# Attention probabilities normalised by the product that turns them, the first head pair's keys and values made in the mixer's last tile, and a new hand-written order of the mixer

## The reference, cut to what matters

```python
q = einsum('bsl,lhe->bshe', rms_norm(c_q), w_uq)          # 64 plain + 32 rotary columns a head
ckv = rms_norm(c_kv); kpe = apply_rope(k_pe)
kv = einsum('bsl,lhe->bshe', ckv, w_ukv)                  # keys (64) and values (64) of each head
s = (q_nope @ k_nope + q_pe @ k_pe) * MLA_SCALE           # 64-token chunks, causal by chunk
o = softmax(s) @ v
...
y, state = wkv_scan(r, decay, k, v, -kk, kk * a, state)   # RWKV-7, tile after tile
```

## Time and the profile before

| | us |
|---|---|
| median of 3 runs | 3215.45 (3214.1 to 3217.09) |
| the profiled execution, its time | 3219.8 |
| its span, first to last instruction | 3217.8 |
| PE busy | 2905.5 (90%) |
| DVE, ACT, POOL busy | 1740.2, 970.5, 529.4 |

### The profile page before, as it was taken

How to read it: one execution, slowest core, us unless ns; L and a number is a source line. 1 busy time by engine, 2 the same in 40 slices (tenths; PEclk the granted TensorE clock), 3 DMA queues, 4 the chain that set the end, 5 groups by cost and what they waited for, 6 DMA issues and landing times. The chain is left out here.

```text
span 3217.8 us, 65907 instructions
## 1 busy us (share of the span) xinstructions
PE 2905.5 (90%) x26600; PEld 2216.2 (69%) x26600; DVE 1740.2 (54%) x3821; ACT 970.5 (30%) x2497; POOL 529.4 (16%) x554
## 2 busy tenths in 40 slices
PE   6999999999999999669999898989976999999990
PEld 6888888888888888545555555545544777777770
DVE  1666666666666666648686877822235222222225
ACT  2333333333333333234343434412220111111115
POOL 0000010000000000000000000001112545555540
PEclk9999999999999999779999999999987999999995
DMA  6121111111121211420101010034325999896447
GB/s 195 34 39 37 37 37 37 38 37 38 37 39 37 39 37 37 100 87 2 39 1 36 4 31 6 1 116 131 127 93 203 289 331 336 268 286 174 101 92 248
DMA packets 337224, 310.21 MB, mean 96 GB/s; under 512 B 235200, under 2 KB 290528, under 8 KB 322528
## 3 DMA queue, kind: packets, MB, share of 16 engines
q1 hardware_dynamic: 315424, 238.88, 24.2%
q0 software_dynamic: 21504, 67.13, 9.1%
HBM read 208.12 MB, written 84.42 MB: 91 GB/s over the span
## 5 line engine op out<-in xcount | busy, mean ns | idle before, releaser
L813 PEld LDWEIGHTS mx_bank<-mx_xT,mx_w_in 128*128 128x128 f32 x5168 | 606.7, 195 | 83.9 <-issue 60.5
L813 PE MATMUL mx_bank<-mx_xT,mx_w_in 128*128 128x128 f32 x5168 | 647.9, 283 | 18.0 <-DVEq L280 14.5
L2310 DVE STREAM_TRANSPOSE ex_xT<-ex_x 128x256 f32<-128x256 f32 x256 | 141.6, 611 | 329.6 <-DMA ex_x<-scr_hx,ex_idx 329.6
L1496 PE MATMUL at_bank<-pl_kT,pl_qT 128*128 128x512 f32 (+5 forms) x656 | 289.9, 528 | 2.3 <-issue 2.3
L1468 ACT ACTIVATE at_PQ<-at_bank,at_nms 128x512 f32<-128x512 f32 (+5 forms) x328 | 192.7, 595 | 253.6 <-DVE at_nms L1596 252.1
L2158 POOL DMA_INDIRECT ex_x<-scr_hx,ex_idx x256 | 244.9, 957 | 114.9 <-issue 76.5
L2241 PE MATMUL ex_gate<-pl_wg,ex_xT 128*128 x1024 | 234.2, 382 | 13.7 <-DVE ex_xT L2310 11.5
L2241 PEld LDWEIGHTS ex_gate<-pl_wg,ex_xT 128*128 128x128 f32 x1024 | 195.8, 192 | 68.7 <-issue 45.0
L2265 PE MATMUL ex_down<-pl_wd,ex_hT 128*128 x512 | 230.3, 593 | 1.5 <-ACT ex_hT L2193 1.5
L2241 PE MATMUL ex_up<-pl_wu,ex_xT 128*128 x1024 | 231.6, 380 | 0.0
L1527 PEld LDWEIGHTS at_bank<-at_PT,at_vals 128*64 128x64 f32 (+1 forms) x2208 | 117.7, 137 | 151.6 <-issue 78.1
(11 more groups left out here) (310 smaller groups left out, 4506.5 us busy)
## 6 DMA issues: line engine op xcount, KB each, us to landing
pl_wg<-in_w_eg SPq DMA_DIRECT2D x32, 1024.0 KB, 6.0
pl_wu<-in_w_eu SPq DMA_DIRECT2D x32, 1024.0 KB, 8.9
pl_wd<-in_w_ed SPq DMA_DIRECT2D x32, 1024.0 KB, 13.7
mx_x<-in_x SPq DMA_DIRECT2D x76, 128.0 KB, 3.8
pl_ro_x<-in_x SPq DMA_DIRECT2D x17, 512.0 KB, 4.1
scr_hx<-ro_h SPq DMA_DIRECT2D x17, 512.0 KB, 2.6
scr_acc<-ro_ha SPq DMA_DIRECT2D x17, 512.0 KB, 3.1
co_r<-scr_acc SPq DMA_DIRECT2D x17, 512.0 KB, 5.7
```

What stands on the lines that cost most here:

```text
L813: ins = pe.matmul(dst, w_in[:, k, col:col + n], xT[:, k, :], start=(k == 0), stop=(k == KC - 1))
L1496: t.mark(pe.matmul(bank[n % SB][:, 0:wd], qT[h][keys(h), j * P:(j + 1) * P], kT[h][keys(h), k0 * P:k0 * P + wd], start=True, stop=True), f ...
L2310: ins = v.transpose(xT[s][:, :, 32 * h:32 * h + 32], x[s][:, h, :].rearrange("p (i k) -> p k i", k=KC))
```

## The change

Three edits. (1) The strings of letters for the mixer are new. (2) `layered` takes another string for the last tile, with a fourth generator d, `first_pair`: PE makes the first pair's keys and values there in banks 0 to 3, ACT and DVE copy them out; `vals` and two memsets move with it, and attention's first turn leaves K0 to V4 out. (3) In attention, the turning of a block becomes a product with a diagonal matrix that holds the reciprocals of the row's sums (`diag`, 4 buffers), so the probabilities are normalised as they are turned; the spreading, `row_rec` and the copy to `recb` go, and `output` is a copy. A chunk is turned at least LAG = 3 steps after its row's last chunk was reached, and its values 3 steps later again; `PQ` has 10 buffers in place of 4.

```diff
-PE_ORDER = ("aacaabcaaaaaaabaaabaaaaaaaaaaaaaaabababbbaabaaababbbabababab"
+PE_ORDER = ("acaaabacaaabaaabaaaaaaaaaaaaaaaabbbbaabaabaaababbbababababab"
...
+LAST_PE_ORDER = "cbc" + "b" * 8 + "ddd" + "bdbdb" + "bd" * 7 + "bddbdbdbdbddbdbb"
+LAST_VEC_ORDER = "cbbbbbbbbcbbbbcbbbbbbcbbbbbbbbbbbbbbbbbbbddbdddb"
...
-        for c in order:
+        for c in last if last is not None and i == count else order:
...
+            g.wait_ge(aten.sem, aten.done(NT - 1, "pr_proj2"))
+            for name in ("kT1", "qT1"):
+                g.memset(ahead.tiles[name][0:32, :], 0.0).then_inc(setup, 1)
...
+            def first_pair(t):
+
+                if t.i < NT - 1:
+                    return
...
+                for n in range(5):
+                    if n == 4:
+                        pe.wait_ge(k_kept, 1)
+                    wd = min(512, KT * P - 512 * n)
+                    for c in range(CKV):
+                        ins = pe.matmul(bank[n % 4][:, 0:wd], w[:, c, 0:P], lat[:, c, 512 * n:512 * n + wd],
+                                        start=(c == 0), stop=(c == CKV - 1))
+                        if c == 0:
+                            yield
+                    ins.then_inc(kv_made, 1)
+                    yield
...
+    for n, c in enumerate(chunks):
+        turn_step[n] = max(row_last[c[:2]] + LAG, turn_step.get(n - 1, -1) + 1)
...
-        step = max(step, place[j, 1, g] + LAG, free)
+        step = max(step, turn_step[place[j, 1, g]] + LAG, free)
...
-            g.memset(kT[1][0:32, :], 0.0).then_inc(setup, 1)
-            g.memset(qT[1][0:32, :], 0.0).then_inc(setup, 1)
-            g.wait_ge(setup, 6)
+            g.wait_ge(setup, 3)
...
             def transposes(t, n):
                 wd, corner = width(n)
-                t.w(act, f"exp{n}")
+                j, h, _ = chunks[n]
+                t.w(vec, f"diag{j}_{h}")
...
-                    ins = pe.transpose(bank[SB + n % TB][0:rows, c:c + P], PQ[:, n % NP, c:c + rows], ident[:, :])
+                    ins = pe.matmul(bank[SB + n % TB][0:rows, c:c + P], PQ[:, n % NP, c:c + rows], diag[:, (2 * j + h) % ND, :],
+                                    start=True, stop=True)
...
-                t.mark(v.tensor_scalar(wide[:, h, :], ones[:], rec[:, 0:1], None, ALU.mult), f"rec_wide{j}_{h}")
+                t.mark(v.tensor_scalar(diag[:, row % ND, :], ident[:], rec[:, 0:1], None, ALU.mult), f"diag{j}_{h}")
...
-                t.w(act, f"rec{j}")
+                t.w(ten, f"PV{j}_{len(groups(j)) - 1}")
...
-                t.mark(v.tensor_tensor(o_sb[:, j, :], bank[7][:, 0:P], recb[:], ALU.mult), f"out_{j}")
+                t.mark(v.tensor_copy(o_sb[:, j, :], bank[7][:, 0:P]), f"out_{j}")
```

More of the change, by code:

```diff
@@ L273, in woven, with layered @@
         run({"b": back(t, False)}, [t], "")
-def layered(eng, count, stages, order):
+def layered(eng, count, stages, order, last=None):
     for _, _, steps, _ in stages:
@@ L1254, in heads_out, with first_pair @@
                 do(v.tensor_tensor(ys[:], ys[:], gk[:], ALU.mult), "gated")
-            layered(v, NT, (("a", 0, avec, project), ("b", 1, vec, rwkv), ("c", 2, ovec, heads_out)), VEC_ORDER)
+            def first_pair(t):
+                if t.i < NT - 1:
+                    return
+                for n in range(5):
+                    v.wait_ge(kv_made, n + 6)
+                    k = min(4, KT - 4 * n)
+                    v.tensor_copy(ahead.tiles["vals"][:, 4 * n:4 * n + k, :],
+                                  bank[(n + 1) % 4][:, 0:k * P].rearrange("p (a n) -> p a n", a=k)).then_inc(v_kept, 1)
+                    yield
+            layered(v, NT, (("a", 0, avec, project), ("b", 1, vec, rwkv), ("c", 2, ovec, heads_out), ("d", 1, None, first_pair)),
+                    VEC_ORDER, LAST_VEC_ORDER)
 def transposed_out(scr):
@@ L1311, in in_order @@
             names += ahead(n + AHEAD) if n + AHEAD < count else []
-            names += before(n) + (at(n) if n < count else []) + after(n)
+            names += before(n) + (at(turned_at[n]) if n in turned_at else []) + after(n)
         return names
@@ L1343, in attention @@
     vec_names += out_names(steps)
-    act_names = KV + [x for n in range(steps + 1) for x in
-                      ([f"exp{n}"] if n < count else []) + ([f"rec{row_end[n - 1]}"] if n - 1 in row_end else [])]
+    act_names = KV + [f"exp{n}" for n in range(count)]
     pol_names = [f"corner{n}" for n in range(count) if width(n)[1]]
@@ L1365, in attention @@
         rec = sb("rec", [P, 1])
-        ones = sb("ones", [P, 64])
-        wide = sb("wide", [P, 2, 64])
-        recb = sb("recb", [P, P])
+        diag = sb("diag", [P, ND, P])
         zero = sb("zero", [P, 64])
@@ L1380, in attention, with given_ahead @@
         last_out = f"out_{NT - 1}"
+        def given_ahead(eng, own, names):
+            assert own.seen == 0 and list(own.names[:len(names)]) == list(names)
+            eng.sem_inc(own.sem, len(names))
+            own.seen = len(names)
         def keys(h):
@@ L1448, in _ @@
         def _(a):
-            a.wait_ge(setup, 6)
+            a.wait_ge(setup, 3)
             def turn(t):
-                for n in range(5):
+                if t.i == 0:
+                    given_ahead(a, act, KV)
+                for n in range(5) if t.i > 0 else ():
                     t.w(ten, f"K{n}")
@@ L1456, in turn @@
                     t.mark(a.activation(kT[1][64:P, 512 * n:512 * n + wd], bank[n][64:P, 0:wd], ACT.Copy), f"K{n}")
-                for n in range(steps + 1):
+                for n in range(count):
                     if n < count:
@@ L1531, in values @@
                             yield
-            def row_rec(t, j):
-                t.w(vec, f"rec_wide{j}_1")
-                t.mark(pe.transpose(bank[7][:, P:2 * P], wide[:].rearrange("p a n -> p (a n)"), ident[:, :]), f"recT{j}")
             def turn(t):
@@ L1541, in turn @@
                 t.w0(act, f"exp{count - 1}")
-                for n in range(5):
+                if t.i == 0:
+                    given_ahead(pe, ten, KV + VV)
+                for n in range(5) if t.i > 0 else ():
                     wd = min(512, KT * P - 512 * n)
@@ L1567, in turn @@
                         next(v)
[L1568 to L1571 removed]
+                    if n in turned_at:
+                        transposes(t, turned_at[n])
                 for _ in v:
```

113 lines of the change are left out of this document (73 added, 40 removed).

## The result

Measured in turns on one chip, the changed kernel took 3280.65 us (median of 4 runs, 3279.27 to 3281.3) and the kernel before 3214.77 us (4 runs, 3213.84 to 3217.09): ratio 1.0203, 95% interval 1.0186 to 1.0221. It is 65.9 us slower. The forecast was 3290 us.

A forecast was written before the change was run, and what follows sets the result against it. PE was taken to bound both mixer and attention. Attention +91, keys and values -21, last tile 0 and mixer's order +5 made +75 us, 3294.8 profiled and 3290 us as median; range 3245 to 3330 us.

The forecast's parts named there:

- The product, +130 us of PE at 0.118 us a block: Attention: turning by a product takes two records, not one, adding 130 us over 1104 blocks; bounds +116 and +166 us.
- The rival of a factor of four: Attention's turning: a product of 0.49 us adds 406 us in place of 130, 3566 us; chance under 0.01.
- a product as cheap as a transpose: Attention's turning: product no dearer than a transpose, so the kernel is faster, -55 us, 3160 us; chance 0.04.
- a product at the price of the earlier trace: Attention: product costs as in the mixer's short run, 0.2725 us, and waits stay 64.5 us; 3355 us; chance 0.07.
- Idle 36 us in the four turns: Attention: PE idle 9 us a turn of the 16 before, 36 in all; bounds 4 and 12 a turn.
- The four turns, 613.8 - 11 + 130 + 36 = 769 us: Attention: PE busy time less row_rec, plus product and idle, against 678.3 us before: +91 us, bounds +57 and +138.
- Keys and values, -21 us: Mixer's end to first scores: making them ahead removes most of 23.0 us; some 1 stays, 1 taken back for clock.
- Last tile, 0 us: Mixer's last tile: keys and values between the recurrence's steps cost nothing, 35 us together against 36.7 now.
- The case of a low clock (+15): Mixer's last tile: if the clock stays low, 7 steps lose 1.2 us each and the values as much again.
- The mixer's order, +5 us: Mixer's tiles: only waits change; a new SA wait adds 8 us, 3 come back; bounds -38.7 (all idle gone), +15.
- The prediction's own sign of error, tiles shorter by over 1 us: Mixer: the prediction said it would be wrong if tiles there shortened by over 1 us.
- Sum: Whole kernel: 91 - 21 + 0 + 5 = +75 us on the profiled 3219.8 us; runs' median 4.35 us lower, 3290 us.

The follow-up runs named there:

- late_transposes: The changed kernel with a transpose in place of each product by the diagonal, attention output left unnormalised; 3181.19 us, ratio 0.9899 to the kernel before.
- no_diagonal: The changed kernel with attention's normalisation as before (transposes, row_rec), so new mixer strings and keys and values made ahead only; 3168.79 us, ratio 0.9845 to the kernel before.
- diagonal_alone: The kernel before with only attention's edit (product with diag, later turning, PQ of 10); 3326.56 us, ratio 1.0339.
- identity_product: The kernel before with only each transpose replaced by a product with the identity, nothing turned later; 3314.1 us, ratio 1.0301.
- first_pair_alone: The kernel before with only the fourth generator and its strings for the last tile, making the first keys and values there; 3194.65 us, ratio 0.994.
- piece_before_SA1: The kernel without the diagonal, with pieces of the queries' projection put back ahead of the second SA and first state_add; 3170.12 us, ratio 0.9861 to the kernel before.
- square_first: The kernel before with kk_norm moved ahead of kpe_sum on PE and its square earlier on ACT; 3193.06 us, ratio 0.9937.

## Why the prediction was right, and where not

It named the direction, and 3290 us was 9 us too high, partly by luck. The lower end of its range also used -5 us for the mixer, which no line of it explains. By its own steps:

- **The product, +130 us of PE at 0.118 us a block.** Right: 127.9 and 131.3 us in two pairs of kernels that differ in it alone, 0.116 and 0.119. The two records of the earlier trace rows were the row to price it by; the short run of the earlier trace rows would have overstated it. The rival of a factor of four falls, and so do the one of a product as cheap as a transpose and the one of a product at the price of the earlier trace rows. The rule of the Trainium skill (Perfetto Trace Analysis, Optimizing Tensor Performance, Transposes) to use the transpose and not a standard product held; the factor of four of the Trainium skill (TensorE: Matmul & The Clock Gate, Terms) is two here, 0.99 us against 0.49 for four blocks.
- **Idle 36 us in the four turns.** 38.5 measured (790.4 - 751.9). The exponentials are in time as forecast. Not forecast was the wait for the diagonal, 22.5 us; it stands where row outputs and `wide` had waited.
- **The four turns, 613.8 - 11 + 130 + 36 = 769 us.** They took 790.4: PE busy 751.9 where 732.8 was charged, idle 38.5 where 36 was. The step that failed is the term left out between -11 and +130: turning late was given no price in PE's work. Counted with the forecast's 11 us for `row_rec`, which no run measures by itself, it is 10 us of PE's time in one pair of kernels (`late_transposes` against `no_diagonal`) and 19 in the other (`diagonal_alone` against `identity_product`). The turns are 10.9 and 13.2 us longer by it. Missing too is 8 us of PE's time that comes with the keys made ahead (621.6 against 613.8 in `no_diagonal`); 5 us of it replaced idle time, and the turns are only 2.6 us longer by it. The two do not add up: PE is busy 749.5 us in `diagonal_alone` and 751.9 with the keys made ahead. The lower clock has a share in both, 34 and 37 us of it in the turns of `late_transposes` and `no_diagonal` against 17 us before. What makes the rest is not explained by a run.
- **Keys and values, -21 us.** -22.6 in the changed kernel. In `first_pair_alone` the first scores come 20.0 us sooner, counted from the seventeenth tile's product for the rotary columns; counted so the changed kernel has 23.1. The 1 us left for small memsets did not show. The clock's price, for which 1 us was taken back, shows inside the turns: the first ten records of scores take 4.18 us in `no_diagonal` and 2.20 before.
- **Last tile, 0 us.** -0.3. With keys and values between the recurrence's steps the granted clock stayed at its upper level from 1317 us to 1365 us, when PE's work in the mixer was done, 1.12 us a step; in `first_pair_alone`, which has no other edit, it did so from 1342 to 1387 us. In the kernel before it fell twice within the recurrence, at 1352 and 1362 us. The case of a low clock (+15) did not come.
- **The mixer's order, +5 us.** Wrong, -28 us, inside the bound of -38.7 set for all idle gone, but not by that way: the listed waits fell by 5 us only, since new ones of 7.3 us came at SA. The step was "the work of a tile is the same; only waits can change": the idle time of the earlier trace rows was priced at its own length and the clock behind it at nothing. Of the 27 us by which the 15 periods shortened, 13.7 are the falls of the clock and 11.1 the second waits. The last 2.2 are the undisturbed tile, 76.1 for 76.25 us, where PE is busy 0.5 us less and waits 0.4 us more. The wait was expected "to move, not to go": the first moved, from `kpe_sum` to `kk_norm`, the second went, and the one at SA came as forecast. (The window holds 15 periods, not the 16 that the prediction counted, which would have made +7 of its +8 us.) The prediction's own sign of error, tiles shorter by over 1 us, is what came: 1.8 us on average.
- **Sum.** Mixer 33 us too high, the turns 22 us too low, the rest 5 us too high: the miss of 15 us in the span is the remainder of two larger ones. Router and experts, taken as unchanged, were 2.8 us shorter; over all profiles here this part takes 1113 to 1117 us whatever the edit, so that is the spread of executions.

The normalisation by a product could not win: it took out 68 small transposes, 11 us of PE by the forecast, and part of 63 us of idle time, and put in 1104 blocks at double price. The other two edits together are 1.5% faster than the kernel before, and `no_diagonal` is the kernel to keep.

## What to carry to other kernels

A transpose fused with a scaling is paid on the engine that bounds the kernel, block by block; count the records of a float32 product of the same shape in the trace before making one of a transpose. A wait on PE costs its length and what the clock does after it: look in the windows for stretches at the lower level, find the waits ahead of them, and merge or fill these first. An order that shortens waits but leaves two of them close together can lose what it won, as `piece_before_SA1` did, so read the tile periods one by one and not their mean.

## What was not expected of the hardware

Adding seven unread products a tile to PE, the engine that bounds the mixer, made the kernel 0.27% faster (interval 0.16% to 0.39%), since they filled waits behind which the clock had fallen. One wait of 1.35 us a tile at that place left the clock at 2.4 GHz in all tiles. In the mixer's full tiles every fall stood where PE waited twice, with 0.4 to 1.4 us of work between: 1.46 us and then 0.24 to 2.27 (seven tiles of the kernel before), 1.19 and then 0.72 or 0.73 (two tiles of `square_first`), 1.34 and then 0.45 to 1.40 (three of `piece_before_SA1`). The clock was then 1.2 GHz for 3.4 or 6.8 us, and the tile 1.8 to 4.4 us longer, the second wait included. But the length of the waits does not tell which tile is hit: five tiles of the kernel before with second waits of 0.14 to 0.87 us and two of `square_first` with 1.27 and 1.29 kept 2.4 GHz. Why is open.
